# An attention loop with three score buffers and scores two pairs ahead, on one core

## The reference

```python
s = jnp.einsum('bqhcd,bkhcd->bhcqk', qb, k).astype(jnp.float32) * scale
bias = jnp.where(dist[None] >= 0, -slopes[:, None, None] * dist[None].astype(jnp.float32), -jnp.inf)
p = jax.nn.softmax(s + bias[None, :, None], axis=-1)
a = p[:, :, 0] - lam * p[:, :, 1]
return jnp.einsum('bhqk,bkhd->bqhd', a.astype(v.dtype), v)
# each head's output: RMS norm over its 128 columns, times (1 - lam_init)
```

## Time and profile before

| | us |
|---|---|
| median of three runs | 3018.17 |
| lowest, highest | 3012.52, 3018.32 |
| the profiled execution | 3015.48 |
| its span, first to last instruction | 3013.7 |
| busy: TensorE, VectorE, ScalarE, GpSimd | 2304.5, 2089.8, 1415.1, 1164.1 |
| mean granted TensorE clock | 0.853 |

### The profile page before, as it was taken

How to read it: one execution, slowest core, us unless ns; L and a number is a source line. 1 busy time by engine, 2 the same in 40 slices (tenths; PEclk the granted TensorE clock), 3 DMA queues, 4 the chain that set the end, 5 groups by cost and what they waited for, 6 DMA issues and landing times.

```text
span 3013.7 us, 36217 instructions
## 1 busy us (share of the span) xinstructions
PE 2304.5 (76%) x11968; PEld 871.7 (29%) x11968; DVE 2089.8 (69%) x5054; ACT 1415.1 (47%) x4057; POOL 1164.1 (39%) x1078
## 2 busy tenths in 40 slices
PE   9878687788788888887767777777777777777766
PEld 6554322223234333332222222222222222222111
DVE  5764566677688797778866666666666666666664
ACT  2135343544555656655644344444444444444443
POOL 1010334443444444444434444444444444444432
PEclk9987898888899999998879789778887898777876
DMA  6011799999999999999999999999999999999997
GB/s 235 29 53 36 305 426 425 426 426 426 424 415 415 423 404 424 411 425 421 420 425 426 427 426 423 426 427 422 426 422 424 423 424 423 427 427 423 424 427 314
DMA packets 174603, 1156.82 MB, mean 384 GB/s; under 512 B 20480, under 2 KB 25152, under 8 KB 40912
## 3 DMA queue, kind: packets, MB, share of 16 engines
q0 software_dynamic: 149168, 1078.73, 85.3%
q1 hardware_dynamic: 25248, 75.79, 6.5%
HBM read 1139.03 MB, written 15.41 MB: 383 GB/s over the span
## 4 chain that ended last, share of the span: by engine, by line
DMA 43%; PE 22%; ACT 11%; DVE 7%; issue 5%; POOL 1%; another core or an unknown queue 0%; DVEq 0%; POOLq 0%; ACTq 0%
DMA ring<-table,e_odd 22%; DMA ring<-table,e_even 21%; PE acc L1844 12%; PE qq_ps L1817 4%; DVE ring L1604 4%; ACT L1424 2%; PE acc L1939 2%; ACT diag L1331 2%; ACT weight L1324 2%; ACT L1317 1%; PE proj L1791 1%; POOL ring L1127 1%; ACT gelu L1424 1%; PE s_ps L1835 1%; DVE y_back L1676 1%
## 5 line engine op out<-in xcount | busy, mean ns | idle before, releaser
L1844 PE MATMUL acc<-ring,diag 64*64 64x512 f32 x8192 | 1301.4, 721 | 625.8 <-ACT diag L1331 601.6
L1604 DVE CUSTOM_DVE_ANT_0 ring<-ring,xn_even 128x1024 f32<-128x1024 f32 x512 | 627.6, 1226 | 390.2 <-DMA ring<-table,e_even 195.8
L1604 DVE CUSTOM_DVE_ANT_0 ring<-ring,xn_odd 128x1024 f32<-128x1024 f32 x512 | 627.1, 1225 | 366.8 <-DMA ring<-table,e_odd 180.5
L1127 POOL DMA_INDIRECT ring<-table,e_even x512 | 570.3, 1114 | 795.2 <-PE acc L1844 723.7
L1127 POOL DMA_INDIRECT ring<-table,e_odd x512 | 567.9, 1109 | 740.9 <-PE acc L1844 695.4
L1424 ACT ACTIVATE gelu<-dots 128x1 f32<-128x1 f32 x1024 | 206.2, 201 | 1185.4 <-DVE dots L1604 1174.0
L1844 PEld LDWEIGHTS acc<-ring,diag 64*64 64x64 f32 x8192 | 248.1, 148 | 1395.6 <-ACT diag L1331 1197.6
L1331 ACT ACTIVATE diag<-pairs,weight 128x64 f32<-128x64 f32 x1024 | 356.5, 348 | 33.4
L1817 PE MATMUL qq_ps<-wq_rest,xnT_cur 128*128 128x256 f32 x736 | 216.6, 432 | 0.0
L1817 PEld LDWEIGHTS qq_ps<-wq_rest,xnT_cur 128*128 128x128 f32 x736 | 142.9, 210 | 144.6 <-issue 127.8
L1324 ACT ACTIVATE weight<-gelu,gate_odd 128x1 f32<-128x1 f32 x512 | 151.1, 295 | 16.7
(11 more groups left out here) (268 smaller groups left out, 2228.3 us busy)
## 6 DMA issues: line engine op xcount, KB each, us to landing
wide<-w_units SPq DMA_DIRECT2D x26, 512.0 KB, 9.2
wq_rest<-wq SPq DMA_DIRECT2D x11, 1024.0 KB, 9.3
ring<-table,e_even POOLq DMA_INDIRECT x512
ring<-table,e_odd POOLq DMA_INDIRECT x512
w_own<-w_units SPq DMA_DIRECT2D x10, 512.0 KB, 6.5
h_next<-x SPq DMA_DIRECT2D x8, 512.0 KB, 17.2
wide<-w_out SPq DMA_DIRECT2D x2, 2048.0 KB, 8.9
wide<-w_out SPq DMA_DIRECT2D x1, 4096.0 KB, 17.3
```

The lines of the kernel that those rows point to most:

```text
L1127: pool.indirect_dma_start(out=ring[:, g % RING, :], out_offset=None, in_=table[:, :], in_offset=bass.IndirectOffsetOnAxis(ap=e_row[m % 2][ ...
L1604: dve.tensor_tensor_reduce(ring[:, g % RING, 0:D], ring[:, g % RING, 0:D], xn[(m // PH) % 2][:], 1.0, 0.0, ALU.mult, ALU.add, dots[:, k:k ...
L1844: ins = pe.matmul(acc[ACC_OF[t]][ROWS[j], HALF[i]], diag[ROWS[i], g % DIAGS, :], ring[ROWS[i], g % RING, D + j * 512:D + (j + 1) * 512], s ...
```

## The change

`z` gets three buffers. The scores of pair `a + 2` are computed ahead of the transposes of pair `a`, and their bias right behind the difference of pair `a`. The exponentials of pair `a + 1` are computed ahead of the copies of pair `a`'s transposed weights. The heads' norms, the fillers, the taps and the convolution's other steps are put into the new lists at the places that the diff shows; tile 0's projection stays where it was, ahead of `output(14)`. `nmax`, `zmax`, `zsum` and `zinv` keep two buffers. No instruction is added or removed. The number of score banks is the same.

```diff
--- before.py
+++ after.py
@@ -95,8 +95,8 @@
         u_pad = [sb("u_even", [P, TAIL + FRONT]), sb("u_odd", [P, TAIL + FRONT])]
         y = [sb("y_even", [P, EARLY * P]), sb("y_odd", [P, EARLY * P])]
         yc = sb("yc", [P, EARLY * P])
-        z_flat = sb("z", [P, 4 * FRONT])
-        z = z_flat[:].rearrange("p (a c n) -> p a c n", a=2, c=2)
+        z_flat = sb("z", [P, 6 * FRONT])
+        z = z_flat[:].rearrange("p (a c n) -> p a c n", a=3, c=2)
         xsq = z_flat[:, 0:2 * FRONT].rearrange("p (a n) -> p a n", a=2)
         dist_i = z_flat[:, 2 * FRONT:2 * FRONT + POS].bitcast(I32)
         zmax = sb("zmax", [P, 2, 2, 3])
@@ -394,7 +394,7 @@
                 nk = META + P * (a % EARLY + 1)
                 act.wait_ge(p_nm, 2 * (a + 1))
                 for c in range(2):
-                    act.activation(z[:, a % 2, c, 0:nk], z[:, a % 2, c, 0:nk], ACT.Exp, scale=SCALE,
+                    act.activation(z[:, a % 3, c, 0:nk], z[:, a % 3, c, 0:nk], ACT.Exp, scale=SCALE,
                                    bias=nmax[:, a % 2, c:c + 1], accum_out=zsum[:, a % 2, c:c + 1]).then_inc(p_exp, 1)
 
             def weights_out(a):
@@ -453,29 +453,31 @@
             channel_roots(2)
             act.wait_ge(p_lam, 3)
             act.activation(lam_s[:, 2:4], lam_s[:, 0:2], ACT.Exp).then_inc(p_lam, 1)
-            for a in range(NU + 1):
-                h, i = divmod(a, EARLY)
-                if a >= 1:
-                    weights_out(a - 1)
-                if i == 1 and h >= 1:
-                    head_root(h - 1)
-                if a < NU:
-                    exponentials(a)
+            def filler(a):
                 if a < len(FILLERS):
                     j, n = FILLERS[a]
                     if j in K:
                         keys(j - K[0], n)
                     else:
                         queries(j - Q[0], n)
-                if a >= 1:
-                    output_out(a - 1)
-                if a == 2:
+
+            exponentials(0)
+            filler(0)
+            for a in range(NU):
+                if a + 1 < NU:
+                    exponentials(a + 1)
+                weights_out(a)
+                if a >= 1 and a % EARLY == 0:
+                    head_root(a // EARLY - 1)
+                filler(a + 1)
+                output_out(a)
+                if a == 1:
                     channel_output(2)
+                elif a == 5:
+                    channel_squares(3)
                 elif a == 6:
-                    channel_squares(3)
-                elif a == 7:
                     channel_roots(3)
-                elif a == 10:
+                elif a == 9:
                     channel_output(3)
             head_root(HEADS - 1)
 
@@ -550,12 +552,12 @@
                 off = (NT - 1 - i) * P
                 if i == 0:
                     dve.wait_ge(p_bias, h + 1)
-                if a >= 2:
-                    dve.wait_ge(p_t, a - 1)
+                if a >= 3:
+                    dve.wait_ge(p_t, a - 2)
                 for n, (lo, hi) in enumerate(chunks(i)):
                     for c in range(2):
                         dve.wait_ge(p_sc, sc_at[a] + 2 * n + c + 1)
-                        dve.tensor_tensor_reduce(z[:, a % 2, c, lo:hi], banks[3 + c][:, 0:hi - lo],
+                        dve.tensor_tensor_reduce(z[:, a % 3, c, lo:hi], banks[3 + c][:, 0:hi - lo],
                                                  bias[:, off + lo:off + hi], 1.0, NEG, ALU.add, ALU.max,
                                                  zmax[:, a % 2, c, n:n + 1]).then_inc(p_z, 1)
                 dve.wait_ge(p_z, sc_at[a + 1])
@@ -574,8 +576,8 @@
                 dve.scalar_tensor_tensor(out=zinv[:, a % 2, 1:2], in0=zinv[:, a % 2, 1:2], scalar=lam_s[:, 1:2],
                                          in1=zsum[:, a % 2, 0:1], op0=ALU.mult, op1=ALU.mult).then_inc(p_inv, 1)
                 dve.wait_ge(p_inv, 2 * a + 2)
-                dve.scalar_tensor_tensor(out=z[:, a % 2, 0, 0:nk], in0=z[:, a % 2, 1, 0:nk],
-                                         scalar=zinv[:, a % 2, 1:2], in1=z[:, a % 2, 0, 0:nk], op0=ALU.mult,
+                dve.scalar_tensor_tensor(out=z[:, a % 3, 0, 0:nk], in0=z[:, a % 3, 1, 0:nk],
+                                         scalar=zinv[:, a % 2, 1:2], in1=z[:, a % 3, 0, 0:nk], op0=ALU.mult,
                                          op1=ALU.add).then_inc(p_a, 1)
 
             def difference_factor():
@@ -640,34 +642,33 @@
             taps(3, 0, 8)
             centre(2)
             taps(3, 8, 16)
-            for a in range(NU + 1):
+            biased(0)
+            difference_factor()
+            biased(1)
+            taps(3, 16, 20)
+            for a in range(NU):
                 h, i = divmod(a, EARLY)
-                if a >= 1:
-                    difference(a - 1)
                 if i == 1 and h >= 1:
-                    head_sums(h - 1)
-                if i == 2 and h >= 1:
                     head_output(h - 1)
-                if a < NU:
-                    biased(a)
-                if i == 3 and h + 1 < HEADS:
+                difference(a)
+                if a + 2 < NU:
+                    biased(a + 2)
+                if i == 1 and h + 1 < HEADS:
                     dve.wait_ge(p_bst, 16)
                     dve.tensor_scalar(bias[:], bias[:], SLOPE0, None, ALU.mult).then_inc(p_bias, 1)
-                if i == 1 and h >= 1:
+                if i == 0 and h >= 1:
+                    head_sums(h - 1)
                     head_scale(h - 1)
                 if a == 0:
-                    taps(3, 16, 20)
-                    difference_factor()
-                elif a == 1:
                     taps(3, 20, 24)
                     divide(2)
+                elif a == 1:
+                    taps(3, 24, 28)
                 elif a == 2:
-                    taps(3, 24, 28)
+                    taps(3, 28, TAPS)
                 elif a == 3:
-                    taps(3, 28, TAPS)
-                elif a == 4:
                     centre(3)
-                elif a == 9:
+                elif a == 8:
                     divide(3)
             head_sums(HEADS - 1)
             head_scale(HEADS - 1)
@@ -769,9 +770,9 @@
                         pe.wait_ge(p_ho, (a - 1) // EARLY)
                 else:
                     wait_evicted(pe, K[1], 1)
-                pe.transpose(banks[7][0:META, 0:P], z[:, a % 2, 0, 0:META], ident[:]).then_inc(p_mt, 1)
+                pe.transpose(banks[7][0:META, 0:P], z[:, a % 3, 0, 0:META], ident[:]).then_inc(p_mt, 1)
                 for b in range(i + 1):
-                    ins = pe.transpose(banks[6][:, b * P:(b + 1) * P], z[:, a % 2, 0, META + b * P:META + (b + 1) * P],
+                    ins = pe.transpose(banks[6][:, b * P:(b + 1) * P], z[:, a % 3, 0, META + b * P:META + (b + 1) * P],
                                        ident[:])
                 ins.then_inc(p_t, 1)
 
@@ -838,27 +839,28 @@
                     seg(j, n)
             group_means(2)
             group_variances(2)
-            for a in range(NU + 1):
+            scores(0)
+            scores(1)
+            seg(*FILLERS[0])
+            for a in range(NU):
                 h, i = divmod(a, EARLY)
-                if a < NU:
-                    scores(a)
-                if a >= 1:
-                    transposes(a - 1)
-                if a < len(FILLERS):
-                    seg(*FILLERS[a])
-                if a == 4:
+                if a + 2 < NU:
+                    scores(a + 2)
+                transposes(a)
+                if a + 1 < len(FILLERS):
+                    seg(*FILLERS[a + 1])
+                if a == 3:
                     group_means(3)
-                elif a == 7:
+                elif a == 6:
                     group_variances(3)
-                if a == NU - 1:
+                if a == NU - 2:
                     for c in range(CG):
                         project_tile_0(HEADS + c, first=(c == 0))
                     project_tile_0(0)
                     project_tile_0(1)
-                if i == 1 and h >= 1:
+                output(a)
+                if i == 0 and h >= 1:
                     transposed_head(h - 1)
-                if a >= 1:
-                    output(a - 1)
             project_tile_0(2)
             transposed_head(HEADS - 1)
             project_tile_0(HEADS - 1, last=True)
```

## The result

The changed kernel takes 3025.7 us (median of six runs, 3024.76 to 3029.79), the kernel before 3015.71 us in the same comparison: a ratio of 1.0036 with a 95% interval of 1.0023 to 1.0048. It is slower by 10 us. 3023 us had been forecast, with 3012 to 3030 as the range, and a chance of 0.44 for "slower by over 0.2%" against 0.46 for "no change"; so the time was met and the sign was left nearly open. As a difference the forecast was +6.3 us, from a base of 3016.8 us; measured are +10.0 us from 3015.71. 1.1 us of the closeness of 3023 to 3025.7 is thus owed to the base and not to the forecast change.

A forecast was written before the change was run, and what follows sets the result against it. The DMA-busy second part starts only after the first, so a microsecond lost in the attention loop counts at the end. Steps of +5.7 us and +0.8 for the clock gave +6.5; from 3016.8 us, 3023 us was forecast, range 3012 to 3030.

The forecast's parts named there:

- the walk: The new order of the loop followed with the old profile's durations: +5.7 us before any clock term.
- The five steps that rest on waits: Pairs 2, 7, 8 and 9, 10, 11 of the attention loop: +1.4, +2.1, -0.95, +4.1, -1.7 us.
- first step: Loop start to pair 1's output: TensorE stands 2 to 4 us in pair 3's scores; +1.1 us.
- third step: Pairs 3 to 6: fillers hide ScalarE's copies and reads, 1.5 us wait in pair 7's scores; +0.05 us.
- The projection: Tile 0's projection after the loop: starts at 291.9 us, before 286.19; from there both programs alike.
- the clock's term: Behind the standstill in pair 3's scores: one slow filler at half a chance, +0.8 us, bounds 0 and 5 us.
- Rival 3: Filler part of the loop: the clock falls there too, three slow fillers add 5 us, 3027 to 3028 us; chance 0.14.
- likeliest case: Whole loop: the new waits outweigh the old, +6.5 us with the clock, 3023 us; chance 0.55.
- Rival 1: Pairs without fillers: the clock stays at its upper level, 1.9 us under before, 3015 us; chance 0.14.
- Rival 2: Whole loop: new waits are hidden and old ones go, 13 us won, 3004 us; chance 0.10.
- Rival 4: Second part: bound by the DMA, it takes the shift in, so nothing changes, 3017 us; chance 0.07.
- The stalls of O(7) and O(10): Outputs of pairs 7 and 10 wait 3.7 and 4.1 us for weight copies queued behind table loads and exponentials.

The follow-up runs named there:

- e5: The changed kernel with nine idle matmuls on TensorE ahead of the second half of pair 3's scores; 3025.6 us, ratio 1.0024.
- g5: f4 with two idle matmuls behind the transposes of each of pairs 7 to 13; 3003.7 us, ratio 0.9958.
- g6: f3 with the same idle matmuls as g5 behind its transposes; 3008.7 us, ratio 0.9973.
- f4: The kernel before, with channel 3's Sqrt, division and Silu moved beside tile 0's projection; 3009.4 us, ratio 0.9972.
- f3: The changed kernel with channel 3's Sqrt, division and Silu beside tile 0's projection, channel 2's division and Silu and three taps later; 3008.4 us, ratio 0.9971.
- e1: The changed kernel with ScalarE's copies of a pair's transposed weights ahead of the next pair's exponentials; 3029.9 us, ratio 1.0040.
- e3: The changed kernel with the first filler ahead of pair 1's scores on TensorE; 3026.2 us, ratio 1.0027.

## Why the prediction was right, and where it was off

Step by step, at the points of the walk, each counted from the first score (before, after):

| point | before | after | step measured | step forecast |
|---|---|---|---|---|
| S(3), O(1) done | 24.9 | 29.6 | +4.7 | +1.1 |
| O(2) and S(4) done | 30.75 | 36.9 | +1.4 | +1.4 |
| O(6) and S(8) done | 59.4 | 67.4 | +1.9 | +0.05 |
| O(7) and S(9) done | 64.35 | 74.5 | +2.1 | +2.1 |
| O(9) and S(11) done | 80.6 | 89.8 | -1.0 | -0.95 |
| O(10) and S(12) done | 84.7 | 98.1 | +4.2 | +4.1 |
| O(11) and S(13) done | 91.55 | 103.2 | -1.7 | -1.7 |
| projection starts | 106.1 | 117.2 | -0.55 | -0.4 |

- **The five steps that rest on waits** (pairs 2, 7, 8 and 9, 10, 11) came within about 0.1 us each, with the forecast waits of 1.1, 3.7, 1.2, 3.6 and 4.1 us measured as 0.94, 3.62, 1.26, 3.61 and 4.08. In one in-order list for each engine the durations of one profile and the semaphores give the new time.
- **The mis-sized term is the clock.** The prediction gave +0.8 us for one slow filler at half a chance and kept three slow ones (5 us) as a rival. Three were slow: 5.72, 4.93 and 4.97 us. In the first step S(1) took 1.50 and the second half of S(3) 1.60 us instead of about 0.7 and 1.06 as well. Followed through: S(1) and the first filler end 1.5 us later than in the walk, S(2) ends 1.3 later, VectorE stands 1.69 us for it, and S(3)'s second half starts 1.7 later. e5 shows that 1.8 us more of this step are owed to the clock at S(3). In the third step the scores, transposes and the filler behind T(5) took 1.6 us longer than in e5, where the filler was fast. That is 1.3 + 1.8 + 1.6 = 4.7 of the 5.5 us by which the first and third steps exceed the forecast.
- **The projection**, which the prediction took as alike, took 12.68 us instead of 11.56. It begins at the lower level in both kernels; before, the clock was back (0.91) 2 us into it, now (0.83) only 4 us into it.
- **How much of the closeness is luck.** In the loop 5.7 us were forecast without the clock's term and 6.5 with it, and 11.1 were measured. Rival 3, at a chance of 0.14, gave 5.7 + 5 = 10.7. So the likeliest case had the places and sizes of the waits nearly right and the whole too small; the time lies in the range because the range was made wide enough for rival 3.
- **Rival 1** (the clock stays up without fillers) did not happen: mean 0.65 from 239 to 296 us. In g5 and g6 added work raised the clock in part of this stretch, and the loop moved by -0.8 and +0.9 us against f4 and f3, which already lack the stalls of channel 3. What the changed kernel itself would gain by the upper clock (the rival's walk said 1.9 us under before) no run shows.
- **Rival 2** (faster) is excluded by the waits of 9.1 us for the copies. **Rival 3** was nearest in mechanism: three fillers were slow, though not the three that it named (the first and those behind T(1) and T(5); of the prediction's three, that of pair 2 took 3.73). Its 3027 to 3028 us and the likeliest case's 3023 stand on either side of 3025.7. **Rival 4** is excluded: the second part took 2701 us as before.
- The rule of the Trainium skill, "ScalarE: Activation LUTs", section "What ACT_TABLE_LOAD costs", of a drain on top of each table load was set aside by the rows, rightly: 269.63 + 1.28 is 270.91, and the Silu starts at 270.93.
- For rival 1 the prediction named the Trainium skill, "TensorE: Matmul & The Clock Gate", section "HAM oscillation — how this bites in real kernels", and the fall around 244 as agreeing. The section speaks of gaps longer than that one of 1.4 us, so this fall bears out the direction only. In the changed kernel the granted clock was still 1.00 from 248 to 252 us and 0.61 in the 4 us behind, after the 3.62 us wait of O(7).
- Two slips in the prediction's words change no step. The old wait of 1.16 us for D(8) is named both at pair 7 and at pairs 8 and 9; by the times it belongs to the latter. And the walk's +6.3 is the difference to the base of 3016.8, while the sum is +6.5.
- The stalls of O(7) and O(10) lie where the prediction put them, behind E, which stands in front of W. That place is no remedy: e1 puts W in front and wins nothing.

Not settled: why the filler behind T(5) is slow behind 1.45 us of idle time in seven profiles and not in two. The changed kernel and e5 have the same busy time of 2.55 us between 228 and 232, and in the next 4 us the granted clock is 0.57 in one and 1.00 in the other.

## What to carry to other kernels

Running one stage further ahead with a third buffer removes the wait for that stage only. When the engines' lists are in order, whatever shares the list with the stage (a table switch, a division) is then in front of something else, so first take out of the lists what can be done where the engines stand anyway: here that gave 8 us, and the third buffer and the second pair ahead nothing. A wait's row names the instruction that came last; moving that instruction up proves a cause only if the sum of all waits falls. Walk the whole new order from one profile's durations, and put the clock into it as a term of its own.

## What the runs showed of the hardware

A standstill of TensorE is paid for a second time by the dense work behind it: behind waits of 2.9 to 4.4 us a filler of eight matmuls took 4.9 to 6.0 us instead of 3.73 (the changed kernel, e3), with the granted clock at 0.50 between 200 and 204 us. Nine idle matmuls in the standstill of S(3) started nothing later by more than 0.2 us and gave 1.8 us in the profile, while the time did not tell them apart. Work added merely to keep the level up paid only in the dense work behind the loop: the projection took 8.75 us instead of 10.57 (g5) and 11.27 (g6), while the loop itself moved by -0.8 and +0.9 us.

A table load took 1.28 us and the next activation started 0.02 us behind its end (269.63, 1.28, 270.93).
